# Seven block products for eight in 14 pairs of input tiles, with the recurrent branch at the end

## The reference

```python
proj = einsum('bsd,de->bse', x, w_in) + b_in                 # 7168 columns: 56 tiles of 128
q, k, v, g_attn, x_rnn, g_rnn, m_attn, m_rnn = split(proj)   # 1024 256 256 1024 1280 1280 1024 1024
attn = window_attention(rope(q), rope(k), v, sink) * silu(g_attn)
xc   = centred_depthwise_conv(x_rnn, conv_w, conv_b)         # width 4
# per direction: r, i = sigmoid(xc @ wa + ba), sigmoid(xc @ wx + bx) in 10 blocks of 128
#   a = exp(-8 r softplus(-lam));  u = sqrt(1 - a^2) * i * xc;  h_t = a_t h_(t-1) + u_t
rnn  = (h_fwd + h_bwd) * silu(g_rnn)
merged = sigmoid(m_attn) * (attn @ w_branch_attn) + sigmoid(m_rnn) * (rnn @ w_branch_rnn)
out = layernorm(alpha * x + merged @ w_out + b_out)
```

## Time and profile before

| | |
|---|---|
| median of 3 runs | 1077.1 us (1075.72 to 1077.69) |
| profiled execution | 1080.0 us, its span 1078.2 us |
| PE busy | 1053.1 us (98%), 4810 matmuls |
| DVE, ACT, POOL busy | 678.9, 397.1, 393.2 us |
| granted clock of PE, mean | 0.995 |

### The profile page before, as it was taken

One profiled execution on the slowest core, in us unless ns is written; L12 is line 12 of the kernel. 1 busy time (PEld: TensorE's weight loads), 2 busy tenths in 40 slices (PEclk: granted clock), 3 DMA queues, 4 the chain that ended last, 5 costly groups with the idle time before them and its releaser, 6 DMA issues.

```text
span 1078.2 us, 12849 instructions
## 1 busy us (share of the span) xinstructions
PE 1053.1 (98%) x4810; PEld 871.0 (81%) x4810; DVE 678.9 (63%) x797; ACT 397.1 (37%) x526; POOL 393.2 (36%) x199
## 2 busy tenths in 40 slices
PE   8999999999999999999999999999999999999996
PEld 6888788888887888878888888888888877888885
DVE  4767877106777754746887887878666333344565
ACT  3133333212334337456466456556520111111012
POOL 3421221332212134453553554355332445435123
PEclk9999999999999999999999999999999999999999
DMA  7210101241010111321211221111031233223412
GB/s 286 58 40 20 39 19 40 98 151 45 20 39 19 30 59 60 127 101 37 59 49 30 68 59 31 48 59 49 20 118 64 99 111 117 78 104 132 174 47 111
DMA packets 22668, 78.56 MB, mean 73 GB/s; under 512 B 2528, under 2 KB 2912, under 8 KB 22496
## 3 DMA queue, kind: packets, MB, share of 16 engines
q1 hardware_dynamic: 20032, 69.48, 19.6%
q10 hardware_dynamic: 2592, 8.48, 2.0%
HBM read 65.36 MB, written 12.58 MB: 72 GB/s over the span
## 4 chain that ended last, share of the span: by engine, by line
PE 85%; DVE 5%; issue 4%; DMA 3%; ACT 1%; POOL 1%; SPq 0%; DVEq 0%; ACTq 0%; POOLq 0%
PE proj L525 22%; PE proj L527 22%; PE proj L526 22%; PE aux L589 2%; DMA raw<-stream 2%; PE aux L526 2%; PE aux L525 2%; PE aux L527 2%; PE aux L571 2%; PE proj L758 1%; PE proj L757 1%; PE aux L758 1%; PE aux L757 1%; PE proj L756 1%; PE aux L756 1%
## 5 line engine op out<-in xcount | busy, mean ns | idle before, releaser
L525 PE MATMUL proj<-xt_hi,w_hi 128*128 128x512 f32 x896 | 357.7, 399 | 5.8 <-POOL w_lo L457 3.8
L527 PE MATMUL proj<-xt_hi,w_lo 128*128 128x512 f32 x896 | 351.1, 392 | 0.0
L526 PE MATMUL proj<-xt_lo,w_hi 128*128 128x512 f32 x896 | 350.8, 392 | 0.0
L454 POOL TENSOR_SCALAR w_hi<-raw 128x1024 fp32r<-128x1024 f32 (+1 forms) x74 | 93.6, 1264 | 576.8 <-PE proj L525 547.7
L457 POOL TENSOR_TENSOR w_lo<-raw,w_hi 128x1024 fp32r<-128x1024 f32 (+1 forms) x74 | 215.8, 2917 | 6.2
L525 PEld LDWEIGHTS proj<-xt_hi,w_hi 128*128 128x128 f32 x896 | 169.2, 189 | 39.2 <-issue 6.4
L527 PEld LDWEIGHTS proj<-xt_hi,w_lo 128*128 128x128 f32 x896 | 169.1, 189 | 36.8
L526 PEld LDWEIGHTS proj<-xt_lo,w_hi 128*128 128x128 f32 x896 | 169.5, 189 | 30.6
L839 ACT ACTIVATE probs<-masked,neg_max 128x385 f32<-128x385 f32 (+1 forms) x64 | 37.9, 592 | 135.9 <-DVE neg_max L1122 135.9
L1044 DVE TENSOR_TENSOR gate_r<-gate_r,racc 128x1024 f32<-128x1024 f32 x8 | 14.7, 1833 | 83.1 <-ACT gate_r L1014 83.1
L527 PE MATMUL proj<-h_hi,w_lo 128*128 128x512 f32 x160 | 62.6, 391 | 0.0
(11 more groups left out here) (140 smaller groups left out, 1711.6 us busy)
## 6 DMA issues: line engine op xcount, KB each, us to landing
raw<-stream SPq DMA_DIRECT2D x80, 512.0 KB, 3.5
spill<-part ACTq DMA_DIRECT2D x16, 512.0 KB, 2.6
attn_in<-spill SPq DMA_DIRECT2D x8, 1024.0 KB, 5.0
x_raw<-x_t SPq DMA_DIRECT2D x8, 512.0 KB, 9.9
rows<-x_rows SPq DMA_DIRECT2D x8, 512.0 KB, 7.4
out<-rows SPq DMA_DIRECT2D x7, 512.0 KB, 2.6
raw<-stream SPq DMA_DIRECT2D x10, 256.0 KB, 2.7
rotary<-tables SPq DMA_DIRECT2D x1, 1024.0 KB, 12.3
```

Of the source, the lines that this page charges most:

```text
L454: nc.gpsimd.tensor_scalar(hi, raw[:, raw_slot, cols], 1.0, 0.0, ALU.mult, ALU.add)\
L525: begun = nc.tensor.matmul(bank, wh, mov_hi, start=first, stop=False)
L526: nc.tensor.matmul(bank, wh, mov_lo, start=False, stop=False)
L527: return begun, nc.tensor.matmul(bank, wl, mov_hi, start=False, stop=last)
```

## The change

*Seven products for eight.* Two tiles of the input projection (x of block b + 2 with g of block b; or the two merge gates of one d) are made as a pair. The sum over 1024 channels is cut into two halves of four tiles, the positions into two halves, and the two tiles are the two rows of a 2 x 2 block product, which is made from seven products of 12 matmuls instead of eight. The weights of three products are units' halves as they are, those of four are sums of halves (`sums`); of the data, four new tiles are used (t1, t2, t4 and t3), made from sums of quarters of x. 14 pairs are made so: one merge pair in block 2, two pairs in each of blocks 3 to 8, one in block 9.

*Sums of weights.* In the attention stage, GpSimd makes the four sums of each pair (`presum_step`), SP loads and stores them to `sums` in HBM.

*Splits.* GpSimd alone splits the 98 half units (512 columns) into hi and lo; it may be three products ahead of PE.

*Copies.* The products of a pair share partial sums. ACT copies a bank four times a pair (`early_copy`), DVE makes four sums a pair (`twin_sum`) and frees the banks.

*Order.* The state of each block is stored to HBM, and the recurrent branch is made at the end: ten units of 48 matmuls over all four pairs of banks, after all pairs. The merge gates go through HBM too. The attention branch's parts, so far added in `merge`, are loaded there (`load_parts`).

In the diff, `load_h(t, ...)` waits for the stored state of block t and is one DMA; `load_parts(d)` is four DMAs of 512 KB and waits from d = 2 on for `parts_gated` of d - 2; `merge_gate` waits for its `twin_sum`, and issues a DMA behind its sigmoid. The diff, cut to its core:

```diff
+PLAIN = 3
+TWINS = [(("merge", 0, 0), ("merge", 0, 1))]
+for _b in range(PLAIN, RNN_BLOCKS):
+    if _b < RNN_BLOCKS - 1:
+        TWINS.append((("x", _b + 2) if _b < RNN_BLOCKS - 2 else ("g", _b + 1), ("g", _b)))
+    TWINS.append((("merge", _b - 2, 0), ("merge", _b - 2, 1)))
...
@@ SP, after the loads of all pairs @@
+            for t in range(4):
+                load_h(t, t // 2)
+            sp.wait_ge(product_split, PRODUCTS)
+            load_unit(NAMES_D[0])
+            load_unit(NAMES_D[1])
+            for t, product in ((4, 3), (5, 3), (6, 4), (7, 4), (8, 4), (9, 4)):
+                load_h(t, product)
+            for n in range(2, 6):
+                load_parts(2 * n - 4)
+                load_parts(2 * n - 3)
+                load_unit(NAMES_D[n])
...
@@ GpSimd @@
+            def split_half(n):
+                pool.wait_ge(half_landed[n % N_SLOTS], 16 * (n // N_SLOTS + 1))
+                if n > 1:
+                    pool.wait_ge(product_begun, max(1, n - 2))
...
+                nc.gpsimd.tensor_scalar(w_slot(n)[0], half_slot(n % N_SLOTS), 1.0, 0.0, ALU.mult, ALU.add)\
+                    .then_inc(half_hi_done, 1)
+                pool.wait_ge(half_hi_done, n + 1)
+                low_weights(n, half_slot(n % N_SLOTS))
...
@@ PE, product i of pair q @@
+                if i == 3:
+                    pe.wait_ge(early_done, 4 * q + 1)
+                    product(q, i, a, t2, False)
...
+                if i == 5:
+                    pe.wait_ge(early_done, 4 * q + 2)
+                    product(q, i, c, b22, False)
+                if i == 6:
+                    pe.wait_ge(early_done, 4 * q + 3)
...
+                    product(q, i, a, t3, False)
...
             for b in range(RNN_BLOCKS):
                 gates(b, 0)
-                branch(b, 0)
+                if b < 2:
+                    branch(b, 0)
+                if b >= PLAIN:
+                    twin_product(merge_of(b) if twin_of(b) is None else twin_of(b), 0)
                 gates(b, 1)
...
@@ ACT, end of block b @@
+                if b == 2:
+                    pad_x(b + 2, FILLS["x", b + 2])
+                if m is not None:
+                    early_copy(m, 0)
+                if q is not None:
+                    sigmoid_of(b)
...
+                if m is not None:
+                    early_copy(m, 1)
+                    if b == 2:
+                        t3_high(0)
+                        t3_high(1)
+                    merge_gate(m, 0)
+                    early_copy(m, 2)
+                    store_state(b)
+                    merge_gate(m, 1)
...
@@ DVE, block b @@
+                if b >= PLAIN:
+                    twin_sum(m - (2 if q is not None else 1), 2)
+                    twin_sum(m - (2 if q is not None else 1), 3)
                 gated_input(b)
-                add(b, 0)
...
+                if q is not None:
+                    twin_sum(q, 0)
+                if b == 2:
+                    t_sums(2)
...
+                if b == 2:
+                    t_low(2)
+                    t_sums(3)
+                if q is not None:
+                    twin_sum(q, 1)
...
                 one_less_decay(b, 1)
+                if b == 2:
+                    t_low(3)
+                if q is not None:
+                    twin_sum(q, 2)
+                    twin_sum(q, 3)
...
                 scan_input(b)
+                if q is not None or last_one:
+                    silu_of(b)
+                if b == 2:
+                    for c in range(2):
+                        t3_sums(c)
+                    for c in range(2):
+                        t3_low(c)
                 scans(b)
+                if m is not None and not last_one:
+                    twin_sum(m, 0)
                 gated_sum(b)
```

More of the change, by code:

```diff
@@ new lines, in columns_b @@
+    place(("merge", 0, 1))
+    place(("rnn", RNN_BLOCKS))
+    place(("rnn", RNN_BLOCKS + 1))
+    for first_d, count, _, before in TILES_C:
+        for d in range(first_d, first_d + count):
+            place(("merge", d, 0))
+            place(("merge", d, 1))
+        for n in (range(before, before + 2) if before < 4 else range(4, 8)):
+            place(("wo", n))
+    return found
+COLS = columns_b()
+NAMES_B = (("x", 1), ("gates", 0), ("attn", 0), ("attn", 1), ("x", 2),
+           ("gates", 1), ("attn", 2), ("attn", 3), ("g", 1), ("x", 3), ("gates", 2), ("g", 2), ("x", 4))
@@ new lines @@
+BRANCH = tuple(("rnn", 2 * (p + 1) + part) for part in range(2) for p in range(PAIRS))
+NAMES_D = BRANCH[:6] + (("wo", 0), BRANCH[6], ("wo", 1), BRANCH[7], ("wo", 2), BRANCH[8], ("wo", 3),
+                        BRANCH[9], ("wo", 4), ("wo", 5), ("wo", 6), ("wo", 7))
+UNITS = {name: UNIT_B + n for n, name in enumerate(NAMES_B + NAMES_D)}
+RING = {name: UNIT_B + n for n, name in enumerate([name for name in NAMES_B if name[0] != "gates"]
+                                                  + list(BRANCH))}
@@ new lines, in source, with branch_bank @@
+def source(n):
+    q, i = divmod(n, 7)
+    if ORDER[i]:
+        unit, half = ORDER[i]
+        return "stream", COLS[TWINS[q][unit]][0] + half * HALF
+    return "sums", (4 * q + SUM_AT[i]) * HALF
+PRESUMS = [[] for _ in range(UNIT_B)]
+_parts = [(q, part) for q in range(len(TWINS)) for part in range(2)]
+for _n, _part in enumerate(_parts):
+    PRESUMS[FIRST_PRESUM + _n * (UNIT_B - FIRST_PRESUM) // len(_parts)].append(_part)
+def branch_bank(b, t):
+    return t % 2 if b == 0 else 1 - t % 2
@@ L477, in _, with twin_weights @@
+            def twin_weights(q, gates_of):
+                for i in range(7):
+                    split_half(7 * q + i)
+                    if i == 3 and gates_of:
+                        gate_weights_half(gates_of)
             for n in range(2):
@@ new lines, in t3_high, with early_copy @@
+            def t3_high(c):
+                act.wait_ge(t3_step, 3 * c + 3)
+                ks = slice(2 * c, 2 * c + 2)
+                copy(t3[0][:, ks, :], t3[3][:, ks, :]).then_inc(t3_hi_done, 1)
+            def early_copy(q, number):
+                i, bank, at = ((0, 0, 0), (1, 2, 1), (3, 0, 2), (6, 0, 0))[number]
+                act.wait_ge(product_done, 7 * q + i + 1)
+                if number == 3:
+                    act.wait_ge(twin_done, 4 * q + 1)
+                elif q:
+                    act.wait_ge(twin_done, 4 * (q - 1) + (4, 3, 2)[number])
+                copy(early[:, at, :], twin_banks(q)[bank]).then_inc(early_done, 1)
@@ new lines, in sigmoid_of @@
+            def sigmoid_of(b):
+                for i in range(2):
+                    act.wait_ge(merge_stored[i], 32 * (b - 2 if b < RNN_BLOCKS - 1 else KT))
+                if b < RNN_BLOCKS - 1:
+                    act.wait_ge(twin_done, 4 * twin_of(b) + 4)
+                    src = silu_g[:, :]
+                else:
+                    act.wait_ge(twin_done, 4 * twin_of(b - 1) + 2)
+                    src = padded[:, CONV_LEFT:CONV_LEFT + SEQ]
+                nc.scalar.activation(stage_out[:, :, :], two(src), ACT.Sigmoid).then_inc(sigm_g_done, 1)
@@ L1342, in _, with gate_parts @@
-            merge(0, 0)
-            for first_d, count, _, _ in TILES_C:
-                with dve.Fori(0, count) as i:
-                    merge(i + first_d, i + (4 + first_d))
+                if b == 1:
+                    t_sums(0)
+                    t_sums(1)
+                    t_low(0)
+                    t_low(1)
+                if m is not None and not last_one:
+                    twin_sum(m, 1)
+            for t in range(4, RNN_BLOCKS):
+                h_low(t)
+            def gate_parts(d):
+                dve.wait_ge(parts_landed[d % 2], 64 * (d // 2 + 1))
+                gate, mine, other = parts(d)
+                tt(mine, mine, other, ALU.add).then_inc(parts_added, 1)
+                dve.wait_ge(parts_added, d + 1)
+                tt(two(mf_hi[d][:, :]), mine, gate, ALU.mult).then_inc(parts_gated, 1)
@@ L1348, in _ @@
+            for d in range(KT):
+                gate_parts(d)
+            for d in range(KT):
+                merge(d)
+                if d % 4:
+                    merged_low(d - 1)
+                if d % 4 == 3:
+                    merged_low(d)
             dve.wait_ge(rows_landed, 16 * NB)
```

818 lines of the change are left out of this document (571 added, 247 removed).

## The result

| | before | after |
|---|---|---|
| median of 4 runs each | 1077.4 us (1075.7 to 1080.0) | 1130.0 us (1129.4 to 1133.2) |
| ratio | | 1.049, 95% interval 1.046 to 1.052 |
| span of the profiled execution | 1078.2 us | 1128.1 us |
| matmuls, PE busy | 4810, 1053.1 us | 4642, 1049.6 us |

4.9% slower, where 1105 us and a range of 1076 to 1130 were forecast. The page of the changed kernel: the engines, then the granted clock in 40 slices, then the chain that ended last by line, and POOL's lower parts of 512 columns (count | busy us, mean ns | idle before).

The account below looks back on a forecast made before the run. TensorE, busy 98% of the span, was taken as the bound, with fewer matmuls helping only as far as other engines follow. -44.6 + 4 + 17 + 24 + 25 + 2 = +27.4 on 1077.1 gave 1104.5, said as 1105 us; range 1076 to 1130.

Parts of the forecast that it names:

- Block 9, branch and end: Block 9 to the last matmul: +25 for waits and the low clock, +2 for the end.
- first stage: Attention stage: GpSimd's 56 weight sums delay DVE's `probs` op, +4 us (bounds 0 and 12).
- the walk: Instruction-by-instruction timing of the engines' queues; put branch unit 2 at 66.7 us, and PE 8 us late in block 2.
- the `probs` waits: First stage: PE has lost 11.5 us to 14 waits for `probs`; perhaps 20 more hit, at 0 to 0.4 us.
- What goes: Whole kernel: 168 matmuls of 0.2267 us (38.1 us) and 6.5 us lost between merge tiles go, -44.6 us.
- Block 2: Transition block: DVE's queue gets 18.1 us more work ahead of the scans, +17 us (bounds 8 and 26).
- two waits of 8 and 10 us: Block 2: PE idles once for 8 us and once for 10 us, at products 1 and 6 of the first pair.
- Blocks 3 to 8: Six recurrent blocks: about 47.5 us each in place of 43.5, +24 us (bounds 0 and 45).
- the copy into `early`: Blocks 3 to 8: PE waits 3.0 us at the merge pair's product 6 for this ACT copy.
- POOL's own sum: Blocks 3 to 8: check from POOL's halves plus DVE's holds, 46.4 to 47.5 us a block.
- the rival that scaled nothing: Blocks 3 to 8: waits as today's means, PE stays fed, +0 there; 1080.5 us, chance 0.18.
- the rival in which POOL is the bound: Blocks 3 to 8: blocks of 51 us, +45, with slower transfers at the end; 1127 us, chance 0.18.

Follow-up runs that it names:

- a_sh64: The changed kernel with its filler at 38 floats instead of 22, so the x tiles and all behind lie 64 bytes higher: 1124.0 us, ratio 1.044.
- a_nosum: a_sh64 with GpSimd's 56 sums of weights cut to 8 of 512 columns each, loads and stores kept: 1117.2 us.
- a_win: a_both with three waits taken, then block 2 reordered on VectorE and ScalarE and branch unit 3 loaded ahead of the parts: 1079.6 us, ratio 1.003.
- a_load: a_sh64 with SP loading the first pair's fourth weight half ahead of block 3's gates' weights: 1127.8 us, ratio 1.048.
- a_win2: a_win with a_load's moved load, outputs 4 and 5 split before VectorE's last scans, 4 to 7 copied before ScalarE's wait for state 9: 1084.3 us, ratio 1.007.
- a_relief: a_sh64 with ScalarE taking 24 of GpSimd's 98 upper parts in blocks 3 to 8, and loads at the end reordered: 1127.2 us, ratio 1.047.
- a_copy: The changed kernel with ScalarE's early_copy(m, 2) ahead of merge_gate(m, 0) in blocks 2 to 8: 1131.5 us, ratio 1.052.
- a_order: a_sh64 with a_copy's edit, and ScalarE's first sigmoids of the next block ahead of the previous pair's two last merge gates: 1117.8 us, ratio 1.038.
- a_both: a_relief and a_order together, plus VectorE merging half the tiles before the last three parts and unit 8 loaded before output weights: 1088.3 us, ratio 1.010.

## Why the prediction came out wrong

The step that failed is the term "Block 9, branch and end", put at +27 and measured at +41.4; the second is the first stage, +4 against +11.7.

- **Block 9, the branch and the end** (+27, measured +41.4). Up to the start of unit 2 the walk was nearly exact: it had unit 2 at 66.7 us after the end of the block's first gates, the trace has it at 67.8; the loss up to there was put at 23 us and is 24.3. Behind it the prediction had 4 us, and the trace has 17.1. Missing were a price for the lower granted clock behind the waits (8.5 us in all; named in the text and given no size), 4.0 us before unit 6 and 3.9 before the output rows in place of 2 and 1.3, and the pace. The pace is 4.2 us in the account, but a_sh64 takes it away and the stage stays at 261.5 us: there the waits come to 32.0 us and the slow steps behind them to 9.1, so waits and clock are what costs here.
- **First stage** (+4, measured +11.7). The sums were mis-sized: 7.8 us by a_nosum, within the bounds of 0 to 12. The path was wrong too: the `probs` waits that I had counted grew by 0.8 us, those for `q_lo` by 7.3. Another 4.8 us up to block 2 are the pace, by a_sh64; without pace and sums the stage is 1 us shorter than before.
- **What goes** (-44.6, measured -46.8): right, 168 matmuls. The pace used for them, 226.7 ns, was not that of the changed kernel. That the kernel's matmuls keep their pace was assumed without being stated: the diff changes the sizes of small tiles, and this moved all large ones. By a_sh64 the pace costs 5 to 6 us here. (The 24 starts from which the prediction took its pace are twelve of the gates and twelve of the branch; they have one shape, and the 226.7 ns are right.)
- **Block 2** (+17, measured +17.7): right in size, in part by luck. The walk put product 1 at 36.5 us after the end of the first gates, and the trace has it at 35.4. But in place of two waits of 8 and 10 us there are four: 2.8 us before the second gates (1.2 in the walk), 4.2 and 3.4 before products 1 and 3, 1.3 before product 6, and slow steps behind them. Product 3 I had not seen. What sets this stage stays open: a_win, a_load and a_win2 fit with DVE's queue.
- **Blocks 3 to 8** (47.5 us predicted, 47.8 measured, 47.7 at the old pace): right in number, and the wait was another one. Named was the copy into `early`; in the trace of the changed kernel the waits are for `w_lo`. The copy's chain is real (a_relief), but stands beside POOL's. POOL's own sum, 46.4 to 47.5, was too high: it works 42.9 us a block and waits 3.4 for PE, a wait that the prediction didn't have. That the two came out at 47 was luck in part. a_copy, a_relief, a_order and a_both show that either bound alone can hardly be moved with profit. POOL's lower parts have means of 1.77 and 1.81 us (the page after, and its second group), near the 1.9 predicted. The price went with the number of POOL's instructions, and the rival that scaled nothing (1080.5) fell. The Trainium skill (SBUF — State Buffer, Who interferes with whom) has the engine that issues first keep the pair for its whole instruction; `w_lo` of 512 columns at 1.29 us with nothing on DVE beside it, 2.15 beside instructions of 1024 columns and 3.11 beside a scan agrees with it.
- The forecast of 1105 missed by 25 us: 14 in the last stage and 8 in the first, under 3 between, less 2 in what goes. The other 3 lie in how the sum was applied: the terms compare traces, the one before was of an execution 2.9 us above its median, the one after of one at its median. The range's upper end, 1130, came from the rival in which POOL is the bound with blocks of 51 us; the time came there by other terms, with blocks of 47.8.

## What to carry to other kernels

Work taken from the busiest engine is worth only what the others can follow. Here two bounds lay within about 1 us of each other: an edit for one of them moved the mean block by -1.0 or +0.5 us, both by -2.6, and with the wait that was left by -3.6. When an edit on the named wait gives nothing, look for the second bound rather than drop the first. An engine that never seems to stop can still be waiting: GpSimd's rows looked full, and 3.4 us of each block were a wait for TensorE. Price a wait twice, once for its length and once for the clock behind it (here 28.7 us of waits and 8.5 behind them). And after any change of buffers compare the pace of a gapless run of matmuls before anything else.

## What the hardware showed

- The time of one 128x512 fp32r matmul hangs on how far the moving tile lies in SBUF from the weights' tile: 226.9 ns at two distances that are multiples of 512 bytes, and 229.0, 232.4 and 233.4 at 64, 128 and 448 bytes above one, at the full granted clock. The last is worth 15 us of 1077. Distances between 128 and 448 were not run.
- The output rows, whose two operands both lie in the part of SBUF that moved, keep 226.6 ns in the changed kernel, with their moving data in the same tile as the slow products.
- Behind a wait of 5.3 us and one of 15.1 us PE's steps are 0.43 us long for a while, at half the granted clock (1.2 GHz), against 0.233.
- PE busy time cannot be compared between two kernels by the number of matmuls alone: 168 fewer made it 3.5 us less, with a slower pace nearly everywhere and stretches at the lower clock.
